# Attention of a hybrid encoder step: the four head pairs written out, and the probabilities-times-values product turned round

## The reference, cut to what matters

```python
z = h @ w_in                       # qa, ka, va, then the columns of retention and gates
s = einsum('bnqhd,bnkhd->bhnqk', qc, kb) * (dh ** -0.5)
s = where(valid, s + bias, -inf)
p = softmax(s, axis=-1)            # exp(s - max) / row sum
o = einsum('bhnqk,bnkhd->bnqhd', p, vb)
...
ya = att @ w_attn_out              # att is o, read by the next projection
```

## Time and profile before

| | us |
|---|---|
| median of 3 runs | 880.26 |
| lowest and highest | 879.74, 881.8 |
| the profiled execution's own time | 880.16 |
| its span, first to last instruction | 878.0 |
| PE busy | 862.4 |
| DVE busy | 481.5 |
| ACT busy | 313.7 |

### The profile page before, as it was taken

How to read it: one execution, slowest core, us unless ns; L and a number is a source line. 1 busy time by engine, 2 the same in 40 slices (tenths; PEclk the granted TensorE clock), 3 DMA queues, 4 the chain that set the end, 5 groups by cost and what they waited for, 6 DMA issues and landing times.

```text
span 878.0 us, 16765 instructions
## 1 busy us (share of the span) xinstructions
PE 862.4 (98%) x6892; PEld 848.4 (97%) x6892; DVE 481.5 (55%) x793; ACT 313.7 (36%) x482; POOL 8.2 (1%) x12
## 2 busy tenths in 40 slices
PE   6999999999999999999999999999999999999996
PEld 6999999999999999999999999999999999999996
DVE  6323576666678577676437665654333443244355
ACT  5211455454441111254446452124212331134342
POOL 1000000000000000000100000000000000000000
PEclk9999999999999999999999999999999999999999
DMA  9322222123221312221241132222223212332202
GB/s 303 97 96 96 75 61 85 59 74 108 78 94 55 103 55 87 65 82 64 94 145 49 50 96 96 91 62 88 96 96 96 90 60 89 96 96 96 89 9 102
DMA packets 77993, 77.30 MB, mean 88 GB/s; under 512 B 2960, under 2 KB 75296, under 8 KB 77952
## 3 DMA queue, kind: packets, MB, share of 16 engines
q1 hardware_dynamic: 68864, 70.53, 24.8%
q10 hardware_dynamic: 8448, 4.02, 1.7%
q0 software_dynamic: 640, 2.17, 0.7%
HBM read 71.70 MB, written 4.99 MB: 87 GB/s over the span
## 4 chain that ended last, share of the span: by engine, by line
PE 96%; DVE 2%; DMA 1%; ACT 1%; issue 0%; DVEq 0%
PE acc L809 75%; PE wk L833 3%; PE wk L809 3%; PE wk L945 3%; PE acc L1068 1%; PE wk L1068 1%; PE acc L1069 1%; PE acc L1070 1%; PE wk L1069 1%; PE wk L1070 1%; PE wk L907 1%; PE wk L906 1%; PE wk L1014 1%; PE wk L1023 1%; DMA ident_sb<-in_ident 1%; PE acc L833 0%
## 5 line engine op out<-in xcount | busy, mean ns | idle before, releaser
L448 ACT ACTIVATE w_hi<-w_raw 128x1024 fp32r<-128x1024 f32 x116 | 123.0, 1060 | 428.2 <-PE acc L809 412.9
L809 PE MATMUL acc<-act_hi,w_hi 128*128 128x272 f32 x1216 | 255.4, 291 | 2.3 <-DVE act_lo L1293 1.2
L809 PE MATMUL acc<-act_hi,w_lo 128*128 128x272 f32 x1216 | 251.7, 288 | 0.0
L809 PE MATMUL acc<-act_lo,w_hi 128*128 128x272 f32 x1216 | 250.8, 288 | 0.0
L809 PEld LDWEIGHTS acc<-act_hi,w_hi 128*128 128x128 f32 x1216 | 191.0, 188 | 6.3 <-issue 2.1
L809 PEld LDWEIGHTS acc<-act_lo,w_hi 128*128 128x128 f32 x1216 | 191.0, 188 | 0.0
L809 PEld LDWEIGHTS acc<-act_hi,w_lo 128*128 128x128 f32 x1216 | 189.9, 189 | 0.0
L1252 DVE TENSOR_TENSOR w_lo<-w_raw,w_hi 128x1024 fp32r<-128x1024 f32 x116 | 141.9, 1223 | 38.5 <-ACT w_hi L448 38.4
L809 PE MATMUL acc<-mid_hi,w_hi 128*128 128x272 f32 x544 | 112.2, 287 | 0.0
L809 PE MATMUL acc<-mid_hi,w_lo 128*128 128x272 f32 x544 | 111.9, 288 | 0.0
L809 PE MATMUL acc<-mid_lo,w_hi 128*128 128x272 f32 x544 | 111.7, 287 | 0.0
(11 more groups left out here) (272 smaller groups left out, 949.0 us busy)
## 6 DMA issues: line engine op xcount, KB each, us to landing
w_raw<-in_w_in SPq DMA_DIRECT2D x44, 512.0 KB, 4.4
w_raw<-in_w_ff_up SPq DMA_DIRECT2D x32, 512.0 KB, 4.5
w_raw<-in_w_ff_down SPq DMA_DIRECT2D x32, 512.0 KB, 4.3
w_raw<-in_w_o SPq DMA_DIRECT2D x8, 512.0 KB, 4.0
x_nat<-in_x_prompt SPq DMA_DIRECT2D x4, 512.0 KB, 5.8
w_raw<-in_w_attn_out SPq DMA_DIRECT2D x4, 512.0 KB, 3.5
w_raw<-in_w_ret_out SPq DMA_DIRECT2D x4, 512.0 KB, 4.5
k_cache<-in_cache_attn_k SPq DMA_DIRECT2D x1, 1024.0 KB, 12.3
```

What stands on the lines that cost most here:

```text
L448: act.activation(w_hi[:, v % 2], w_raw[:, v // 2, :, P * (v % 2):P * (v % 2) + P], ACT.Copy).then_inc(hi_ready, 1)
L809: ins = pe.matmul(dst[:, n, 0:HALF], w[:, k, :], h[:, k, HALF * n:HALF * n + HALF], start=begin, stop=end)
```

## The change

The pairs are written out (plain Python loops, no loop registers). The copies `k_pair` and `v_pair` go; the transposes and splits read `z`. The values are split into high and low fp32r halves that lie beside each other (`v_stack`, 128 columns: high, low of head 0; low, high of head 1) and are the stationary operand; the transposed probabilities, split into `p_hi` (ACT) and `p_lo` (DVE), are the moving one, up to 512 columns at a time. The result is transposed already: one half of the partitions holds the product with the high values, the other half that with the low values. ACT copies the low half's rows to `att_low`, and DVE adds them into `z`. The sample's product stays as it was. The inverse row sums are turned from a column into a row spread over 64 partitions by two DMAs of POOL, through DRAM (`inv_dram`), for each head, and DVE applies them later (`normalise`). The five transposes of `att_nat` are replaced by one of the sample (`sample_transposed`).

```diff
 # POOL
-            pool.wait_ge(scores_mm, 2 * PAIRS)
...
+            for h in range(AH):
+                if h == AH - 1:
+                    pool.wait_ge(scores_mm, 2 * PAIRS)
...
+                pool.wait_ge(inv_ready, h + 1)
+                pool.dma_start(inv_dram[h].rearrange("(t p) -> p t", p=P), row_inv[:, 0:4], allow_slow_non_contiguous=True).then_inc(inv_out, 16)
+                if h % 2 == 0 and h:
+                    pool.wait_ge(attT_ready, h // 2)
+                pool.wait_ge(inv_out, 16 * h + 16)
+                pool.dma_start(inv_spread[AD * (h % 2):AD * (h % 2) + AD, :], bass.AP(inv_dram.tensor, SEQ * h, [[0, AD], [1, SEQ]]))\
+                    .then_inc(inv_in, 16)
 # PE
-                        v = v_nat[:, b, AD * e:AD * e + AD] if t < 4 else v_cache[:, b, AD * e:AD * e + AD]
-                        ins = pe.matmul(out, probsT[:, PT_COL[t] + n * b:PT_COL[t] + n * b + n], v,
-                                        start=(b == 0), stop=(t < 4 and b == blocks - 1))
...
+                for b in (0, 1, 3, 2):
+                    if b < 3:
+                        pe.wait_ge(p_hi_ready, 3 * h + b + 1)
+                        pe.wait_ge(p_lo_ready, 3 * h + b + 1)
+                    v = v_stack[:, b, 2 * e:2 * e + 2, :].rearrange("p n c -> p (n c)")
+                    cols = slice(PT_COL[b], PT_COL[b] + SEQ - P * b)
+                    pe.matmul(wk[:, PV_COL + P * b:PV_COL + SEQ], v, p_hi[:, cols], start=(b == 0), stop=False)
+                    ins = pe.matmul(wk[:, PV_COL + P * b:PV_COL + SEQ], v, p_lo[:, cols], start=False, stop=(b == 2))
...
+            def second_head(i):
...
+                    if k == 3:
+                        probs_transposes(i, 1)
+                    if k == 5:
+                        probs_times_v(i, 1)
...
+            def first_head(i):
...
+                    if k == 7:
+                        probs_transposes(i, 0)
...
+            def between_heads(i):
...
+                    if k == 1:
+                        probs_times_v(i, 0)
+                    if k == 3:
+                        pe.wait_ge(k_stacked, 2 * i + 2)
+                        scores(i, 1)
...
+                column_tile(g, 0, act_hi, act_lo, before=second_head(i - 1) if i else None)
...
+                column_tile(g, 2, act_hi, act_lo, before=first_head(i))
+                column_tile(g, 3, act_hi, act_lo, before=between_heads(i))
 # DVE
+            def normalise(i):
+
+                dve.wait_ge(att_added, 2 * i + 2)
+                dve.wait_ge(inv_in, 32 * i + 32)
+                dve.tensor_tensor(z[:, i, 0:SEQ], z[:, i, 0:SEQ], inv_spread[:], ALU.mult).then_inc(attT_ready, 1)
...
+            for i in range(PAIRS):
+                g = G_RET + i
+                if i:
+                    masked_max(i - 1, 1)
+                    to_z(g - 1, 3, Z_RQ + 4 * i - 1)
+                queries_low(i)
+                if i:
+                    split_ahead(g - 1, 3)
+                    row_inverse(i - 1, 1)
+                    probs_low(i - 1, 1)
                 keys_low(i, 0)
+                if i:
+                    att_add(i - 1, 1)
                 to_z(g, 0, Z_RQ + 4 * i)
                 split_ahead(g, 0)
+                if i:
+                    normalise(i - 1)
+                values_low(i)
                 to_z(g, 1, Z_RQ + 4 * i + 1)
+                split_ahead(g, 1)
                 masked_max(i, 0)
+                keys_low(i, 1)
+                row_inverse(i, 0)
+                probs_low(i, 0)
                 to_z(g, 2, Z_RQ + 4 * i + 2)
+                att_add(i, 0)
                 split_ahead(g, 2)
...
+            rotate_cross(Z_RK, 0)
+            split_ahead(G_GATE - 1, 3)
+            row_inverse(PAIRS - 1, 1)
+            probs_low(PAIRS - 1, 1)
+            rotate_add(Z_RK, 0, k_rotated)
+            att_add(PAIRS - 1, 1)
```

More of the change, by code:

```diff
@@ new lines, in stack_keys_low, with queries_high @@
+            def stack_keys_low(i, e):
+                rows, others = slice(AD * e, AD * e + AD), slice(AD - AD * e, 2 * AD - AD * e)
+                act.wait_ge(k_lo_ready, 2 * i + e + 1)
+                act.activation(k_stack_lo[others, :], k_stack_lo[rows, :].bitcast(fp), ACT.Copy).then_inc(k_stacked, 1)
+            def queries_high(i):
+                if i:
+                    act.wait_ge(scores_mm, 2 * i)
+                for e in range(2):
+                    rows = slice(AD * e, AD * e + AD)
+                    act.activation(q_stack[rows, e, :], z[rows, i, :], ACT.Copy, scale=AD ** -0.5).then_inc(q_hi_ready, 1)
@@ L949, in probs_times_v @@
                 ins.then_inc(pv_mm, 1)
+                out = wk[0:DEC, PV_SAMPLE:PV_SAMPLE + AD]
+                for b in range(4):
+                    pe.matmul(out, p_sample[:, DEC * b:DEC * b + DEC], v_cache[:, b, AD * e:AD * e + AD], start=(b == 0), stop=False)
+                pe.matmul(out, p_sample[0:DEC, 4 * DEC:5 * DEC], v_nat[0:DEC, 4, AD * e:AD * e + AD], start=False, stop=True).then_inc(pv_mm, 1)
             def to_natural(src, col):
@@ L1040, in _ @@
                 last = u == 4 * RH - 1
-                column_tile(G_GATE + u // 4, u % 4, act_hi, act_lo, half_used=h_half_used if last else None)
+                between = {0: second_head(PAIRS - 1), 1: sample_transposed(PAIRS - 1, rv_nat_ready, 1)}.get(u)
+                column_tile(G_GATE + u // 4, u % 4, act_hi, act_lo, before=between, half_used=h_half_used if last else None)
                 for i in range(RH):
@@ L1323, in _, with queries_low @@
             order.flatten()
+            def queries_low(i):
+                for e in range(2):
+                    rows, others = slice(AD * e, AD * e + AD), slice(AD - AD * e, 2 * AD - AD * e)
+                    dve.wait_ge(q_hi_ready, 2 * i + e + 1)
+                    dve.scalar_tensor_tensor(q_stack[others, e, :], z[rows, i, :], AD ** -0.5, q_stack[rows, e, :].bitcast(fp),
+                                             ALU.mult, ALU.subtract).then_inc(q_lo_ready, 1)
             def keys_low(i, e):
@@ new lines, in att_add @@
+            def att_add(i, e):
+                h = 2 * i + e
+                rows = slice(AD * e, AD * e + AD)
+                dve.wait_ge(att_low_ready, h + 1)
+                dve.tensor_tensor(z[rows, i, 0:SEQ], wk[rows, PV_COL:PV_COL + SEQ], att_low[rows, :], ALU.add)
+                dve.wait_ge(pv_mm, 2 * h + 2)
+                dve.wait_ge(inv_ready, h + 1)
+                if e == 0 and i:
+                    dve.wait_ge(att_tr, i)
+                dve.tensor_scalar(att_sample[0:DEC, AD * e:AD * e + AD], wk[0:DEC, PV_SAMPLE:PV_SAMPLE + AD], row_inv[0:DEC, 4:5], None, ALU.mult)\
+                    .then_inc(att_added, 1)
@@ L1488, in _ @@
                 to_z(g, j, Z_GATE + u)
+                if u == 1:
+                    normalise(PAIRS - 1)
                 for i in range(RH):
```

323 lines of the change are left out of this document (170 added, 153 removed).

## The result

The changed kernel takes **888.96 us** (median of 6 runs, 888.02 to 894.29) against 880.7 for the kernel before on the same chip (6 runs, 879.74 to 881.8): the ratio is 1.0102, interval 1.008 to 1.0124. It is slower by 1%, where 0.9% faster was forecast. The profiled execution took 888.43 us.

What follows compares the result with a forecast made beforehand. PE, busy 98% of the span, was taken as the bound: 880.16 - 10.2 of PE work + 1.0 + 0.4 + 0.9 of waits = 872.3, with 0.1 and 0.3 added 872.7 us; own range 870.8 to 874.8, overall 870.2 to 877.2.

Steps and rivals of the forecast that it cites:

- (e): DVE's normalise waits for POOL's two DMAs of inverses; bounds 5.8 to 11.8 us, taken as 8 to 9, hidden.
- The slack: Time from issue to landing the two inverse DMAs may take before DVE's next to_z and maxima get late: 11.5 us.
- Rival 1: POOL's round trip shows: above 11.5 us, normalise is late and PE waits ahead of first heads' transposes, pairs 1 to 3; 13%.
- (a): First heads: DVE makes w_lo first, so PE waits 0.25 us for the fourth exponential, four times: 1.0 us.
- The product: Attention product per head on PE: eight fp32r matmuls, 1.36 us instead of 2.37; 8.0 us less for eight heads.
- The way back: Five att_nat transposes per pair, 0.74 us and about 0.1, become one at 0.3: 2.2 us less in all.
- (b): Second heads of pairs 0 to 2: DVE's p_lo just fits PE's product; 0 to 0.1 us each, taken as nothing.
- (c): Last head: DVE waits for POOL's loads and rotates before p_lo, so PE waits 0.4 us at the product.
- (d): Behind the last head: ACT's and DVE's work makes PE wait about 0.9 us ahead of the first retention scores.

Runs made afterwards that it cites:

- experiment 6: Changed kernel with the inverses turned on DVE in 32 x 32 blocks and written as 128 runs of 128 bytes, order kept: 873.43 us, ratio 0.9929.
- Experiment 9: Changed kernel with 16, 23 and 29 zero-operand PE matmuls filling the stalls ahead of first heads' transposes, pairs 1 to 3: 884.01 us, ratio 1.0043.
- experiment 7: experiment 6 with first heads' maxima ahead of the weights' low half, and the first query rotation right behind the first gate tile: 872.18 us, ratio 0.9903.
- experiment 1: Changed kernel with normalise of pairs 0 to 2 moved on DVE behind keys_low(i, 1) of the next pair: 878.63 us, ratio 0.9968.
- experiment 8: Useless DVE reductions ahead of first heads' maxima, pairs 1 to 3: five on experiment 2, 889.33 us; two on experiment 6, 877.12; five on experiment 6, 889.32.
- experiment 10: experiment 6 plus, behind each read back, 512 pieces of 4 bytes written by POOL to DRAM nobody reads: 880.57 us, ratio 0.9999.
- experiment 2: experiment 1 with POOL's three retention loads issued ahead of its wait for head 6's inverses to land: 876.52 us, ratio 0.9941.
- experiment 3: Changed kernel with inv_dram written as 128 runs of 16 bytes, not 512 of 4 (scales by other rows' inverses): 873.34 us, ratio 0.9905.
- experiment 5: Changed kernel with the 512 single elements of each head's inverses sent from ACT's queue instead of POOL's: 893.94 us in its one run.

## Why the prediction was wrong, point by point

**The step that failed is (e)**, "`normalise` waits for POOL's two DMAs ... I take 8 to 9 ...: hidden". It took 15.2 us for pair 1's second head (14.6 and 16.1 for those of pairs 0 and 2). The bounds, 5.8 to 11.8, were made from four transfers with rows of 512 bytes and more, and none of them had single elements. The row that was nearest in bytes was not nearest in what costs. The slack itself was estimated at 11.5 us; 15.2 less a stall of 2.8 makes it 12.4. With the write in 128 pieces the two DMAs need 8.3, as taken, and the kernel takes 873.3 to 873.4 us against the 872.7 forecast, inside the forecast's own range. That the 8 to 9 fit a quick write was luck as far as this kernel goes: its own write was not of that kind. Two signs that had been named for being wrong both came: DVE idle ahead of `z<-z,inv_spread`, released by a DMA, and the two landings over 11.5 together (9.6 + 3.7).

The runs give the price that those rows could not, by the count of pieces: 9.6, 5.1 and 2.8 us for 512, 256 and 128, about 18 ns for each. That a piece is small doesn't make the write slow by itself: 128 pieces of 16 bytes (2.8) and of 128 bytes (3.6) both land quickly.

**Rival 1 was the right mechanism** at 13%: "microsecond for microsecond" ahead of the first heads of pairs 1 to 3, decided by DVE's `inv_spread`. It foresaw 883 at 15 us. The 6 us to 889 are **a term that the sum didn't have**: the clock behind a stall. The sum can be closed between the end of the first scores and the end of the last. In the changed kernel:

```profile
109.19 0.41 PE L868 MATMUL acc<-act_hi,w_hi 128*128 128x272 f32 x2
...
249.54 0.41 PE L868 MATMUL acc<-act_hi,w_hi 128*128 128x272 f32 x2
```

and in experiment 6:

```profile
108.06 0.41 PE L869 MATMUL acc<-act_hi,w_hi 128*128 128x272 f32 x2
...
234.26 0.41 PE L869 MATMUL acc<-act_hi,w_hi 128*128 128x272 f32 x2
```

140.35 us against 126.20, so 14.15 more. The three waits are 8.55, of which about 0.25 each is (a) and stands in experiment 6 too, so 7.8. The clock is the rest: PE's busy time in the windows from 154 to 160, 196 to 200 and 238 to 244 us, times what the granted clock lacks of 1.00, is 6.1 (an estimate). Experiment 9 gives 5.0 by the medians. Of the 15.4 us between the two profiled executions another 1.1 stand ahead of the first scores, where the change does nothing. There the changed kernel's execution has a stretch of lower clock of its own (busy times and clock as above; experiment 6 and the kernel before have 1.00 there):

```profile
0.00:20.00 20.00, 12.41 (x77) 11.72 (x78) 13.33 (x22) 12.96 (x19) 2.62 (x8) 0.91 0.98 306
```

The three stalls grow (2.0, 2.9, 3.7) as the way from POOL's first issue to the multiplication grows (14.6, 15.2, 16.1). Why that grows isn't settled.

Why the clock falls with an idle PE isn't shown. That it does is read from the windows: in the changed kernel it is granted at 0.50 or 0.51 behind each of the three stalls, and with the stalls filled (experiment 9) at 1.00. The prediction priced no stall with it, since before there was none.

**The product**: 1.36 forecast, 1.36 measured. Inside, the pair of 128 columns took 0.17 (174.66 - 174.49) and not 0.22, that is 0.085 for each, inside the forecast's bounds of 0.06 and 0.17 and under the 0.11 that was taken. What is left for the change of format is 0.15 and not 0.1: the total came out by two small errors that cancel.

**The way back**: 0.3 forecast for the one transpose. In the changed kernel the rows around it are these:

```profile
140.78 0.41 PE L868 MATMUL acc<-act_lo,w_hi 128*128 128x272 f32 x2
141.03 0.41 PE L868 MATMUL acc<-act_hi,w_lo 128*128 128x272 f32 x2
141.38 0.24 PE L892 MATMUL wk<-ident_sb,att_sample 32*128 32x32 f32 x1
141.55 0.52 PE L868 MATMUL acc<-act_hi,w_hi 128*128 128x272 f32 x2
```

141.55 - 141.03 is 0.52, and such a row costs 0.25, so 0.27.

**(a)**: 0.25 for each first head. Experiments 6 and 7 differ by 0.20 ahead of the transposes, and by some 0.05 within them. It was right. Of it, the 0.1 for waking PE was an estimate, and 0.05 to 0.06 is what the traces show (pair 2's fourth exponential is read out at 195.70 in the changed kernel and at 188.07 in experiment 6, and PE starts at 195.75 and 188.13). **(b)**: nothing, and no such wait is listed. **(c)**: 0.4, measured 0.6 in the changed kernel and 0.5 in experiment 6. **(d)**: 0.9, measured 0.8. A pair takes 182.68 - 145.36 = 37.3 us in experiment 6 from the end of its first scores to the end of the next pair's, "about 37" where it took 39.3.

**What the chances missed.** The terms of PE, DVE and ACT were each right to 0.2 us, and were outweighed by one that had bounds from the wrong kind of row. The bounds were 5.8 to 11.8 and the true value lay 3.4 above them. The price for being over the edge was also not the excess alone: to 8.6 us of waits came another 5 to 6 by the clock.

## What to carry to other kernels

Count the pieces of a small DMA, not its bytes (2 KB took 2.8 us in 128 pieces and 9.6 in 512), and expect them to delay what other queues have under way (`v_cache` 8.2 for 2.9). Before a column of values is sent through DRAM one element at a time, turn it on an engine: 0.21 us of DVE saved 15 us here. Nothing that waits for a DMA should stand in an engine's queue ahead of work that PE is about to need, if a place behind it does as well (10.3 us came back by it in experiment 1). And a stall of PE of some microseconds can cost more than its length (9.0 us of stalls cost 15.9 in experiment 8), while a short one (1.2 us here) didn't.

## What the hardware showed that was not expected

- 512 writes of 4 bytes to DRAM land in 9.6 us, 256 of 8 bytes in 5.1, 128 of 16 in 2.8; issued from ACT's queue, the 512 take 8.7.
- While they are in flight, other transfers land 1.6 to 6 us later, whoever waits for them (`v_cache` 8.2 for 2.9 before, `state_in` 8.6 for 4.4 and `out_new_k_prompt` 8.4 for 2.4 in experiment 10, `out_new_v_prompt` 4.0 for 2.4).
- One issue of a small store by ACT took 4.03 us in experiments 1 and 2 and 3.10 in the changed kernel, beside 0.52 in experiment 3, and ACT's next instructions came behind it.
- A granted clock of 0.50 or 0.51 for PE in one or more windows of 2 us behind stalls of 2.0 us and more in the changed kernel (and 0.50, 0.54 and 0.50 behind those of 3.1, 2.7 and 4.6 in the last head of experiments 1, 2 and 10), but 1.00 behind one of 2.39 in experiment 8, and behind those of 1.2. No length of the stall parts the two cases here.
- Near 14 to 20 us, while the inputs are loading, some profiled executions have PE at a granted clock of 0.50 (the changed kernel from 16 to 18, experiments 5 and 7 from 14 to 20) and others at 1.00 (the kernel before, experiments 3, 6 and 9).
